# Second layer's output projection of a two-layer hybrid backbone: seven block products for eight on the latent tokens, weight sums made by accumulating transfers, a ring of four weight halves

## The reference, cut to what matters

```python
    o = jnp.concatenate([jax.nn.silu(g_c) * multiscale_pool(...), jax.nn.silu(g_d) * spatial_gating(...)], axis=-1)
    x = x + gate * rmsnorm(o @ w_out[l], norm_post[l])
```

## Time and profile before

| | us |
|---|---|
| median of 3 runs | 1113.85 |
| span of the profiled execution, first to last instruction | 1113.0 |
| TensorE busy | 1091.5 |
| VectorE busy | 705.0 |
| ScalarE busy | 427.3 |
| GpSimd busy | 33.4 |
| last four chunks, TensorE's first to last matmul issue | 971.16 to 1104.88 |

### The profile page before, as it was taken

One profiled execution on the slowest core, in us unless ns is written; L12 is line 12 of the kernel. 1 busy time (PEld: TensorE's weight loads), 2 busy tenths in 40 slices (PEclk: granted clock), 3 DMA queues, 4 the chain that ended last, 5 costly groups with the idle time before them and its releaser, 6 DMA issues.

```text
span 1113.0 us, 13620 instructions
## 1 busy us (share of the span) xinstructions
PE 1091.5 (98%) x5356; PEld 879.1 (79%) x5356; DVE 705.0 (63%) x1029; ACT 427.3 (38%) x693; POOL 33.4 (3%) x66
## 2 busy tenths in 40 slices
PE   6999999999999999999999999999999999999997
PEld 5576687887878878888888788888888888888885
DVE  4555575767677787699966645487665766343335
ACT  4333334433636432243346852223423223243332
POOL 1000010000000000000010000000000000000000
PEclk8999999999999999999999999999999999999999
DMA  9998866454545567567884235345644554433423
GB/s 381 407 394 337 339 242 250 166 228 162 216 193 214 211 272 303 228 236 295 315 325 153 83 145 188 135 170 190 211 172 184 210 206 159 183 133 132 155 72 114
DMA packets 39327, 242.28 MB, mean 218 GB/s; under 512 B 4784, under 2 KB 4896, under 8 KB 13408
## 3 DMA queue, kind: packets, MB, share of 16 engines
q1 hardware_dynamic: 29232, 190.85, 44.8%
q0 software_dynamic: 7344, 46.29, 11.5%
q10 hardware_dynamic: 2688, 4.26, 1.4%
HBM read 237.67 MB, written 3.72 MB: 217 GB/s over the span
## 4 chain that ended last, share of the span: by engine, by line
PE 95%; DVE 2%; ACT 1%; DMA 1%; issue 1%; DVEq 0%; ACTq 0%; SPq 0%
PE bank L966 27%; PE bank L968 26%; PE bank L967 26%; PE bank L1030 3%; PE bank L1112 2%; PE bank L1051 1%; PE bank L1176 1%; PE bank L1128 1%; PE bank L1091 1%; PE bank L1135 1%; DMA x_t<-in_x_turned 1%; PE bank L917 1%; PE bank L915 1%; PE bank L916 1%; PE bank L1101 0%
## 5 line engine op out<-in xcount | busy, mean ns | idle before, releaser
L966 PE MATMUL bank<-w_hi,h_op 128*128 128x512 f32 x1114 | 450.0, 404 | 2.6 <-DVE h_op L1761 2.2
L968 PE MATMUL bank<-w_hi,h_op 128*128 128x512 f32 x1114 | 435.4, 391 | 0.0
L967 PE MATMUL bank<-w_lo,h_op 128*128 128x512 f32 x1114 | 434.5, 390 | 0.0
L1509 DVE TENSOR_TENSOR w_lo<-raw,w_hi 128x1024 fp32r<-128x1024 f32 x200 | 244.3, 1222 | 191.3 <-ACT w_hi L1221 190.9
L1221 ACT ACTIVATE w_hi<-raw 128x1024 fp32r<-128x1024 f32 x200 | 210.0, 1056 | 227.3 <-PE bank L968 211.8
L966 PEld LDWEIGHTS bank<-w_hi,h_op 128*128 128x128 f32 x1114 | 209.4, 188 | 58.0 <-issue 15.6
L968 PEld LDWEIGHTS bank<-w_hi,h_op 128*128 128x128 f32 x1114 | 209.1, 188 | 45.2
L967 PEld LDWEIGHTS bank<-w_lo,h_op 128*128 128x128 f32 x1114 | 209.6, 188 | 39.5
L966 PE MATMUL bank<-w_hi,o_low 128*128 128x512 f32 x192 | 75.8, 395 | 0.0
L968 PE MATMUL bank<-w_hi,o_low 128*128 128x512 f32 x192 | 74.9, 390 | 0.0
L967 PE MATMUL bank<-w_lo,o_low 128*128 128x512 f32 x192 | 74.8, 390 | 0.0
(11 more groups left out here) (227 smaller groups left out, 929.8 us busy)
## 6 DMA issues: line engine op xcount, KB each, us to landing
raw<-in_w_in SPq DMA_DIRECT2D x68, 1024.0 KB, 5.3
dot_raw<-in_ada_tiles POOLq DMA_DIRECT2D x32, 1024.0 KB, 5.1
raw<-in_w_out SPq DMA_DIRECT2D x32, 1024.0 KB, 4.9
raw_first<-in_ada_first SPq DMA_DIRECT2D x21, 1024.0 KB, 11.1
raw<-in_ada_groups SPq DMA_DIRECT2D x16, 1024.0 KB, 6.7
raw<-in_ada_halves SPq DMA_DIRECT2D x16, 1024.0 KB, 4.7
open_raw<-in_w_in SPq DMA_DIRECT2D x24, 512.0 KB, 11.5
dot_raw<-in_ada_first SPq DMA_DIRECT2D x11, 1024.0 KB, 10.1
```

Source lines behind the costliest of these rows:

```text
L966: pe.matmul(out, operand(layer, kind, 0, k, t), hi, start=k == begin, stop=False)
L967: pe.matmul(out, operand(layer, kind, 0, k, t), lo, start=False, stop=False)
L968: last = pe.matmul(out, operand(layer, kind, 1, k, t), hi, start=False, stop=k == end)
L1509: dve.tensor_tensor(w_lo[:, half % WRING, :, :].rearrange("p k n -> p (k n)"), src, hi, ALU.subtract)\
```

## The change

The four chunks become two pairs of chunks (`PAIRS`). For the latent tiles 1 and 2, a pair is a product of a 2 x 2 block matrix (two token tiles by two halves of 1024 rows, A11, A12, A22 and so on) with a 2 x 2 block matrix of weights (two halves of rows by two chunks: b11, b21, b12, b22). It is made in seven block products instead of eight, in Winograd's arrangement. The combined token blocks (H1, H3, G, E) are made once, by four VectorE additions or subtractions over a full-precision copy `o_full`, and then rounded by ScalarE and split by VectorE (`combine`, `part_combined`). The combined weight blocks are made in place: t1 in the raw slot of b11, t2 on t1, t4 on t2, t3 on b22, each by GpSimd issuing a transfer from DRAM with `accum_op=ALU.add`, in 16 transfers of 512 KB a pair (`add_weights`). The context tile takes part with the same weight blocks (its rows a1 and a2), and stays at four block products.

A pair has 28 halves, in the order b11 (4 halves), b21 (4), t1 (4), then t2 and b22 in turn (8), then t3 and t4 in turn (8). A half of b11, b21, t1 or b22 feeds two block sums (12 matmuls), one of t2, t3 or t4 feeds one (6). A pair is 56 steps in the table. Some partial sums are copied out of PSUM by ScalarE (`keep`, 5 a pair) and added to or subtracted from banks by VectorE (`join`, 6 a pair with the one called `rest`). The entry `take` squares a finished bank on ScalarE and multiplies it by the gate row on VectorE. The ring gets a fourth slot in these pairs (`w_late`), and rounding and splitting go three halves ahead. In the last pair the residuals of tiles 0 and 1 stand at steps 46 and 50, and tile 2 comes after the last matmul; `tile_steps` is no longer used here. SyncE loads three block pieces of a pair (b11, b21, b22), 6 transfers of 1 MB for 8 before.

```diff
+
+PAIRS = [(L1 + N_IN + 2 * n, L1 + N_IN + 2 * n + 1) for n in range(2)]
+PAIR_OF = {c: p for p, pair in enumerate(PAIRS) for c in pair}
+FIRST_PAIR, LAST_PAIR = PAIRS[0][0], len(PAIRS) - 1
+PAIR_STEPS = 28
+STEPS = [PAIR_STEPS if c in PAIR_OF else KT for c in range(len(CHUNKS))]
+HALF_KT = KT // 2
+UPS = HALF_KT // 2
+PAIR_SEQ = [(op, u) for op in ("b11", "b21", "t1") for u in range(UPS)]
+PAIR_SEQ += [(op, u) for u in range(UPS) for op in ("t2", "b22")]
+PAIR_SEQ += [(op, u) for u in range(UPS) for op in ("t3", "t4")]
+PAIR_SUMS = {"b11": (("W", "a1", True), ("X", "A11", True)), "b21": (("Z", "A12", True), ("W", "a2", False)),
+             "t1": (("Y", "H1", True), ("V", "a1", True)), "t2": (("X", "G", False),),
+             "b22": (("V", "a2", False), ("Y", "E", False)), "t3": (("S", "H3", True),), "t4": (("X", "A22", False),)}
+PAIR_OUT = [(0, 0, "W", "b21"), (0, 1, "Z", "b21"), (1, 0, "V", "b22"), (1, 1, "Y", "b22"), (1, 2, "S", "t3"),
+            (0, 2, "X", "t4")]
+KEPT_SUMS = (("W", "b11"), ("X", "b11"), ("Y", "t1"), ("X", "t2"), ("S", "t3"))
+KEEP_W, KEEP_P1, KEEP_Y, KEEP_U2, KEEP_P7 = range(5)
+JOINS = {1: 1, 2: 2, 3: 3, "rest": 4, 4: 5, 5: 6}
+ROLE_NEED = ("W", "X", "Z", "Y", "V", "S")
+LATE_SLOT = 3
 
...
+
+def w_before(half):
+    return half - WRING if half < PAIR_HALF + WRING else half - WRING - 1
 
 UNITS = [[(c, h)] for c, h in HALVES if c < FIRST]
-UNITS += [[(c, h), (c, h + 1)] for c, h in HALVES if c >= FIRST and h % 2 == 0]
+UNITS += [[(c, h), (c, h + 1)] for c, h in HALVES if c >= FIRST and c not in PAIR_OF and h % 2 == 0]
 NTH_UNIT = {ch: n for n, unit in enumerate(UNITS) for ch in unit}
 
 STAYS = []
...
+    pre(FIRST_PAIR, "round", PAIR_HALF + 2)
+    pre(FIRST_PAIR, "split", PAIR_HALF + 2)
+    for i, entry in ((10, "H1"), (13, "H3"), (14, "G"), (18, "E")):
+        put(FIRST_PAIR, i, "combine", entry)
+    for i, entry in ((11, "H1"), (15, "G"), (19, "E"), (28, "H3")):
+        put(FIRST_PAIR, i, "part_combined", entry)
+    for p, (c, _) in enumerate(PAIRS):
+        for i, n in ((3, 0), (4, 1), (5, 2), (20, 3)):
+            put(c, i, "pair_gate", p, n)
+        for i, n in ((8, KEEP_W), (9, KEEP_P1), (24, KEEP_Y), (38, KEEP_U2), (54, KEEP_P7)):
+            put(c, i, "keep", p, n)
+        for i, n in ((17, 1), (40, 2), (41, 3), (42, "rest"), (54, 4)):
+            put(c, i, "join", p, n)
+        for i, n in ((16, 0), (18, 1), (41, 2), (42, 3), (55, 4)):
+            put(c, i, "take", p, n)
+        if p < LAST_PAIR:
+            put(c, 56, "join", p, 5)
+            put(c, 57, "take", p, 5)
+    p, c = LAST_PAIR, PAIRS[-1][0]
+    put(c, 10, "table_end")
+    for i, t in ((20, 0), (21, 1)):
+        put(c, i, "y_sum", t)
+    for i, t in ((44, 0), (45, 1)):
+        put(c, i, "y_end", t)
+    for i, t in ((46, 0), (50, 1)):
+        put(c, i, "residual", t)
+    pre(len(CHUNKS), "y_sum", 2)
+    pre(len(CHUNKS), "join", p, 5)
+    pre(len(CHUNKS), "take", p, 5)
+    pre(len(CHUNKS), "y_end", 2)
+    pre(len(CHUNKS), "residual", 2)
...
-                half = NTH_HALF[p[1], p[2] // 2] + 2
+                half = NTH_HALF[p[1], p[2] // 2] + (3 if p[1] in PAIR_OF else 2)
...
+        def pair_source(p, op, u):
+
+            start = {"b21": "b21", "b22": "b22", "t3": "b22"}.get(op, "b11")
+            return raw[:, pair_slot[p, start, u // 2], u % 2 * 2 * CW:(u % 2 + 1) * 2 * CW]
...
+            for p, (c, _) in enumerate(PAIRS):
+                layer, _, col = CHUNKS[c]
+                for op in ("b11", "b21", "b22"):
+                    for v in range(2):
+                        slot = pair_slot[p, op, v]
+                        if op == "b22":
+
+                            sp.wait_ge(lo_ready, pair_half(p, "b21", 2 * v + 1) + 1)
+                        elif p:
+
+                            sp.wait_ge(lo_ready, pair_half(p - 1, "t3" if op == "b11" else "t4", 2 * v + 1) + 1)
+                        else:
+
+                            wait_used(ring[len(ring) - RAW + 2 * (op == "b21") + v])
+                        w = w_out[layer, col // CW + (op == "b22")]
+                        k = 4 * v + (0 if op == "b11" else HALF_KT)
+                        sp.dma_start(raw[:, slot, :], w[:, k * CW:(k + 4) * CW]).then_inc(raw_in[slot], 16)
...
+            def add_weights(p, op, u):
+
+                source, side, low = {"t1": ("b11", 1, 0), "t2": ("t1", 1, HALF_KT), "t3": ("b22", 1, 0),
+                                     "t4": ("t2", 0, HALF_KT)}[op]
+                pool.wait_ge(lo_ready, pair_half(p, source, u) + 1)
+                layer, _, col = CHUNKS[PAIRS[p][side]]
+                k = low + 2 * u
+                pool.dma_start(pair_source(p, op, u), w_out[layer, col // CW][:, k * CW:(k + 2) * CW],
+                               accum_op=ALU.add).then_inc((grown_c if op == "t3" else grown_a)[u], 16)
+
+            for p in range(len(PAIRS)):
+                for op in ("t1", "t2"):
+                    for u in range(UPS):
+                        add_weights(p, op, u)
+                for u in range(UPS):
+                    add_weights(p, "t4", u)
+                    add_weights(p, "t3", u)
...
+            def pair_step(c, s):
+
+                half = NTH_HALF[c, s // 2]
+                p, op, u = of_pair(half)
+                sums = PAIR_SUMS[op]
+                if s % 2 == 0:
+
+                    pe.wait_ge(lo_ready, half + 1)
+                if len(sums) == 2:
+                    work = [(sums[s % 2], j) for j in (2 * u, 2 * u + 1)]
+                else:
+                    work = [(sums[0], 2 * u + s % 2)]
+                for (role, name, begins), j in work:
+                    if j == 0:
+                        if begins:
+
+                            wait_acc(pe, *holder[p, role])
+                        else:
+
+                            n = {("W", "b21"): KEEP_W, ("X", "t2"): KEEP_P1, ("Y", "b22"): KEEP_Y, ("X", "t4"): KEEP_U2}\
+                                .get((role, op))
+                            if n is not None:
+                                wait_kept(pe, p, n)
+                        if name in nth_combined:
+                            pe.wait_ge(combined_ready, nth_combined[name])
+                    if p == 0 and op in ("b11", "b21"):
+                        wait_free(pe, "o", 1, j + (HALF_KT if op == "b21" else 0))
+                    out = bank[roles[p][role]][:, :]
+                    hi, lo = (w[:, j % 2, :] for w in w_parts(half))
+                    pe.matmul(out, pair_operand(name, 0, j), hi, start=begins and j == 0, stop=False, skip_group_check=True)
+                    pe.matmul(out, pair_operand(name, 0, j), lo, start=False, stop=False, skip_group_check=True)
+                    last = pe.matmul(out, pair_operand(name, 1, j), hi, start=False, stop=j == HALF_KT - 1,
+                                     skip_group_check=True)
+                if s % 2:
+                    last.then_inc(mm_done, 1)
...
+                elif what == "keep":
+                    p, n = e[1:]
+                    role, op = KEPT_SUMS[n]
+                    wait_stage(act, p, op)
...
+                    act.activation(kept_place(p, n), bank[roles[p][role]][:, :], ACT.Copy).then_inc(kept, 1)
...
+                elif what == "combine":
+                    a, op, b, out = {"H1": (1, ALU.subtract, 3, 3), "H3": (0, ALU.subtract, 1, 1),
+                                     "G": (3, ALU.subtract, 0, 0), "E": (2, ALU.add, 0, 2)}[e[1]]
+                    dve.wait_ge(op_hi, nth_op("o", 1, KT - 1) + 1)
+                    if e[1] in ("G", "E"):
+
+                        dve.wait_ge(combined_full, 2 if e[1] == "G" else 3)
+                    dve.tensor_tensor(o_full[:, out, :, :], o_full[:, a, :, :], o_full[:, b, :, :], op)\
...
+                elif what == "join":
...
+                    _, _, role, op = PAIR_OUT[n]
+                    out = bank[roles[p][role]][:, :]
+                    other, sign = {1: (KEEP_P1, ALU.add), 2: (KEEP_W, ALU.subtract), 3: (KEEP_U2, ALU.subtract),
+                                   4: (KEEP_Y, ALU.subtract), 5: (KEEP_P7, ALU.add)}[n]
+                    wait_stage(dve, p, op)
+                    wait_kept(dve, p, other)
+                    if n == 4:
+                        wait_kept(dve, p, KEEP_P7)
+                        wait_joined(dve, p, "rest")
+                        dve.tensor_tensor(out, kept_place(p, other), out, sign).then_inc(joined, 1)
+                    else:
+                        dve.tensor_tensor(out, out, kept_place(p, other), sign).then_inc(joined, 1)
...
+                    dve.wait_ge(y_squared, TOKS * N_OUT + nth_take[c, t] + 1)
...
+                    dve.tensor_tensor(mixed[:, t, col:col + CW], acc(c, t)[:, :], gate_row, ALU.mult).then_inc(taken, 1)
```

255 lines of the change are left out of this document (214 added, 41 removed).

## The result

The changed kernel takes 1118.62 us, median of 4 runs (1118.45 to 1118.80), beside 1113.82 us for the kernel before (4 runs, 1113.64 to 1113.89). The ratio is 1.0044, with an interval of 1.0029 to 1.0059: slower by 4.8 us. The forecast was slower by 2.8 us.

What follows compares the result with a forecast made beforehand. The prediction took TensorE to bound the kernel, with VectorE's queue holding it after the change. -10.9 + 8.6 - 0.2 + 4.8 + 0.5 = +2.8 us gave 1116.6 us, range 1110 to 1127, the forecast's own 1113.5 to 1120.

Steps and rivals of the forecast that it cites:

- wait gone: In the stage: the one wait of TensorE for a split in the kernel before, taken off the sum, -0.2 us.
- additions: wait before half 26: Adding transfers: near twice a plain transfer's engine time, mostly hidden, with a little lateness costing +0.5 us.
- tail: From the last matmul to the last VectorE instruction: 9.3 us where 4.5 stood, +4.8 us.
- Place one: Start of the first pair: ScalarE late with the copy of W, so TensorE's first b21 half waits 0.7 us.
- place two: Steps 9 to 19: VectorE's combinations delay the split of half 12, TensorE waits 2.0 us.
- place three: Middle of t3/t4: joins, takes and last-pair residual between splits make TensorE wait 1.7 + 4.2 = 5.9 us.
- two-passes rival: Adding transfers take two passes and fill the engines, 66.6 us a pair against 65: 1119 to 1127 us, chance 0.17.
- One after the other: Rival: additions served singly, 16 a pair of 5 us or more, TensorE waiting some 20 us: 1150 us and more, 0.08.
- The faster one: Rival: queues hold TensorE less than walked, under 3.8 us of waits: 1110 to 1111.5 us, chance 0.20.
- Even: Rival: waits at the first pair's start and steps 9 to 19 vanish, the end stays: 1113.9 us, chance 0.05.
- named as right: Signs: 528 matmuls at 0.227 us, some 8 us waiting for `w_lo`, VectorE over 90% busy there, 9 us at the end.
- named as wrong: Signs: roundings waiting for a DMA, a t3/t4 half with no gap ahead, under 7 us after the last matmul.

Runs made afterwards that it cites:

- e1: Changed kernel with the 16 GpSimd transfers a pair overwriting the slot instead of adding (weight sums left out): 1113.82 us.
- e3: Changed kernel with the weight ring back to three slots and rounding and splitting two halves ahead: 1120.47 us.
- e2: Changed kernel with tile 0's residual moved from step 46 to step 50 of the last pair, behind the last split: 1118.54 us.
- e10: Changed kernel without the residuals of tiles 0 and 1, their stores held to the places where the changed kernel makes them: 1114.80 us.
- e9: Changed kernel with 11 small filler products on TensorE ahead of the first pair's half 26: 1116.89 us.
- e8: Changed kernel with plain transfers instead of adding ones and without the residuals of tiles 0 and 1: 1110.03 us.
- e5: Changed kernel with SyncE's first load of the second pair held until the first pair's last t3 addition has landed: 1116.77 us.
- e7: Changed kernel without the residuals of tiles 0 and 1, their stores having nothing to wait for: 1119.20 us.
- e11: Changed kernel with the second pair's first load held only until the last t4 addition has landed: 1115.70 us.

## Why the prediction was right, and which term was mis-sized

The direction and the range held: 1118.62 lies 2.0 us above 1116.6. That the sum came so near is in part luck. The forecast had the slowdown come from VectorE's queue, -10.9 + 8.6 - 0.2 + 4.8 = +2.3 us, with 0.5 for the additions; e1, where the transfers don't add, measures what is left without the adding at +0.1 us, and the adding at 4.8. So all but the adding was priced 2.2 us too high and the adding 4.3 too low. The queues and the longer end do eat the 10.9 us that the matmuls save, as forecast; what makes the kernel slower than before is the adding. The terms:

| term | forecast | measured |
|---|---|---|
| 48 matmuls less | -10.9 | -10.9 |
| TensorE waits for VectorE's and ScalarE's queues | +8.6 | +5.9 |
| wait gone | -0.2 | -0.2 |
| additions: wait before half 26 | +0.5 | +3.1 |
| half clock behind the two longest waits | none | +3.3 |
| second matmul 0.1 us late behind each other wait | none | +0.5 |
| pace of the other matmuls, 0.2295 for 0.2271 us | none | +1.2 |
| tail | +4.8 | +2.4 |
| last store | 0 | -0.4 |
| sum | +2.8 | +4.9 |

The medians differ by 4.8.

**Matmuls.** 176 x 3 = 528 are in the trace of the stage (counts 84, 44, 28 and 20 of line L1166), as forecast. Their pace away from waits, turnings and half clock is 0.2295 us from start to start instead of 0.2271. e1 has 0.2292, so it isn't the adding. It goes with the fourth slot: 0.2339 us after a matmul on a weight in `w_late`, 0.2280 after the others, and e3, which has no fourth slot, is at 0.2277. So "the matmuls keep shape and type, so the pace stays" left out where the weight stands: some 0.9 of the 1.2 us. Why a weight in `w_late` is read more slowly no run tells.

**Queues.** Place one was under-sized (1.6 for 0.7), place two over-sized (0.4 for 2.0), and place three over-sized in both pairs (3.0 for 4.2 in the last, 0.8 for 1.7 in the first). e1 shows these waits without the additions. e2 shows that the last of them isn't worth its length in time: VectorE's queue sets the end whether TensorE waits in it or not.

**Tail.** Counted from the last split the forecast held, 10.3 for 10.9 us. (Its own 10.9 less 1.4 us for TensorE's last half is 9.5, not 9.3, so the term should have read +5.0.) Counted from the last matmul it was too long, because TensorE ran its last halves at half clock behind the 2.2 us wait, beside VectorE. That half clock (1.7 of the 3.3 us) and the shorter tail are one thing seen from two sides: wait, half clock and tail at the end together are VectorE's queue. So the terms of the end can't be priced alone; e10 prices the two VectorE residuals in it at 3.8 us together.

**Additions.** This is the step that was mis-sized: "that with a little lateness costs 0.5 us". e1 prices it at 4.8 us, 3.1 of waiting and 1.6 of half clock behind it (e9 took 1.7 back by filler). The reading of near twice a plain transfer's engine time was right: 5.3 us a megabyte against 3.1 for the same bytes in e1 and 2.8 in the earlier trace rows. What failed is the conclusion from it. The engine time was compared over the whole pair, 66.6 us against a pair of 65, and taken as hidden; but the sum can't be spread evenly, since a pair's additions are freed by splits that come in a burst. In the burst from 1000 to 1031 us the engines are at 0.99 (0.63 in e1), and from 1008 on each addition takes longer to land than the one before it (5.4 and 5.7 us for those issued at 994 and 996, 6.4 at 1008.1, 8.9 at 1010.6, 12.0 at 1014.9, 15.3 at 1019.1), and the last one, on which half 26 hangs, gets the whole backlog. The slack of 11 to 21 us for t3 and t4 was used up by this.

That is the mechanism of the two-passes rival, at its rate near 200 GB/s; it cost TensorE time in the first pair alone. In the last pair the t1 additions land in 11 to 17 us, beside three loads issued within 1.2 us, and the later ones in 8 to 11; ScalarE's roundings wait for them three times (3.8, 1.1 and 1.2 us between 1048 and 1068), but TensorE has no wait from 1043 to 1095 us. The Trainium skill ("Collectives: The Full Stack", the part on the bandwidth ceiling) gives the adding step of a ring collective half a copy's rate. This trace, of an addition into SBUF and no collective, agrees: 5.3 for 2.8 us of engine time a megabyte, 1.9 times, and 1.7 times against e1's 3.1.

**The other rivals.** One after the other fell: 31 additions of 9.3 us would be 288 us in a stage of 137, so two and more are in flight at a time. The faster one's condition, under 3.8 us of waits, was met neither in the changed kernel nor in e1 (5.9 us); only e8, without two residuals, got under it. Even is what e1 came to, with the end unchanged in its kind but the waits not gone.

**The signs.** Of those named as right, 528 matmuls and VectorE over 90% busy at the end (10.53 of 10.60 us) came, and waits for `w_lo` of some 8 us, but 3 of these are the addition's; the pace and the 9 us tail did not. Two of those named as wrong came: roundings that wait for a DMA (9.8 us), and a tail under 7 us, by a hair (1106.59 to 1113.54).

## What to carry to other kernels

When a change trades TensorE's work for another engine's or a queue's, walk the burst and not the mean: transfer engines that are at 0.88 over a stage can be at 0.99 for 30 us of it, and the item at the end of the burst pays for all. A megabyte added into SBUF by a transfer cost the engines here 1.7 to 1.9 plain ones, so count it as two before deciding that it hides. Take out the change's new ingredient alone before crediting a total that fits, for a sum can come near with its terms wrong both ways. And price a stall of TensorE with what follows it, here half the clock for nine matmuls, and the end of the program by the queue that ends last, since work moved within that queue gives nothing.

## What the runs showed of the hardware that was not expected

- Behind waits of 2.2 and 3.1 us TensorE's matmuls came 0.43 us apart for nine of them, then 0.23 again; behind one of them this began at once, behind the other after three matmuls. In e5 a 1.9 us wait did it too; in e7 one of 2.1 us at 1095 did not, nor did waits of 2.3 us in the last pair of e5 and of e11 (granted clock 1.00 from 1096 to 1106 and to 1104 us). In e3 it began five matmuls behind a wait of 2.3 us, and in e2 twelve matmuls were slow behind the first pair's wait. Waits of 0.4 to 0.8 us in the changed kernel were never followed by it. With 11 small products in the 3.1 us wait (e9) it did not come there.
- GpSimd needs 0.85 us to issue an adding transfer and 0.53 us for the same transfer without adding (medians 845 and 531 ns).
- SyncE's plain loads suffer beside the additions: 9.0 us for 1 MB in this stage, 5.5 in e1 with plain transfers beside them, 4.8 before.
- TensorE's step is 0.234 us after a matmul on a weight in the fourth slot and 0.228 after one in the other three, with the same shapes.
- GpSimd scales a 128 x 2048 tile in 5.9 to 7.3 us and adds 128 x 512 in 1.26 us, 1.7 beside VectorE's residual, whose 128 x 512 pieces then take 1.7 and once 4.2 us instead of 0.75.
